# Around the expert loops of a two-block kernel: where the output store is awaited, where the gate is multiplied, and when the next weights are asked for

## The reference

```python
# each layer
x = x + gate_msa * attention(modulate(rms_norm(x)))
h = modulate(rms_norm(x))
g_idx = argmax(h @ w_group + b_group)                 # one group of 8 experts
top_v, top_i = top_k(e_logits[g_idx], 2)              # two experts inside it
weights = g_prob[g_idx] * softmax(top_v)              # w1, w2 per token
# expert_dispatch: assignments sorted by expert, padded to blocks
hid = silu(xb @ w_gate[e]) * (xb @ w_up[e])           # 1024 -> 512
ys  = hid @ w_down[e]                                 # 512 -> 1024
y[token] = w1 * ys[slot1] + w2 * ys[slot2]
x = x + gate_mlp * y
# after both layers
out = rms_norm(x) * final_norm_g
```

## Time and profile before

| | |
|---|---|
| median of 3 runs | 2659.88 us (2655.5 to 2660.84) |
| the profiled execution, its time | 2657.06 us |
| its span, first to last instruction | 2655.1 us |
| PE busy | 2244.2 us, 85% of the span |
| PEld busy | 996.6 us, 38% |
| DVE busy | 591.2 us, 22% |
| ACT busy | 563.8 us, 21% |
| POOL busy | 184.6 us, 7% |
| mean granted TensorE clock | 0.923 of full speed |
| HBM traffic | 235 GB/s over the span |

### The profile page before, as it was taken

One profiled execution on the slowest core, in us unless ns is written; L12 is line 12 of the kernel. 1 busy time (PEld: TensorE's weight loads), 2 busy tenths in 40 slices (PEclk: granted clock), 3 DMA queues, 4 the chain that ended last, 5 costly groups with the idle time before them and its releaser, 6 DMA issues. The chain is left out here.

```text
span 2655.1 us, 21739 instructions
## 1 busy us (share of the span) xinstructions
PE 2244.2 (85%) x8350; PEld 996.6 (38%) x8350; DVE 591.2 (22%) x1288; ACT 563.8 (21%) x932; POOL 184.6 (7%) x364
## 2 busy tenths in 40 slices
PE   8999999999999987848887787499799488878782
PEld 4454544444444444422222222244454222222220
DVE  2364421221020055310000000210562200100003
ACT  2223310010020043211111111200781111112111
POOL 3130020000000012010000000100120100000001
PEclk9999999999999998868889999799899588899996
DMA  7478649113222030159999999610003399999994
GB/s 246 166 264 302 225 162 390 47 63 106 84 80 90 0 127 16 64 217 429 428 428 429 427 429 422 223 63 0 32 17 134 142 427 429 428 428 428 429 429 165
DMA packets 133673, 624.84 MB, mean 235 GB/s; under 512 B 14212, under 2 KB 25868, under 8 KB 109036
## 3 DMA queue, kind: packets, MB, share of 16 engines
q1 hardware_dynamic: 114912, 557.11, 52.1%
q0 software_dynamic: 13488, 49.86, 5.0%
q10 hardware_dynamic: 5212, 17.05, 1.6%
HBM read 571.31 MB, written 52.67 MB: 235 GB/s over the span
## 5 line engine op out<-in xcount | busy, mean ns | idle before, releaser
L1754 PE MATMUL ps<-ring,arena 128*64 128x512 f32 x2048 | 516.0, 666 | 134.7 <-ACT arena L1782 115.4
L221 PE MATMUL ps<-hT,ring 128*128 128x512 f32 (+3 forms) x1328 | 560.3, 584 | 4.2 <-issue 4.2
L221 PEld LDWEIGHTS ps<-hT,ring 128*128 128x128 f32 (+1 forms) x1328 | 249.2, 190 | 313.6 <-issue 309.7
L1754 PEld LDWEIGHTS ps<-ring,arena 128*64 128x64 f32 x2048 | 160.7, 153 | 468.3 <-issue 387.8
L1769 PE MATMUL ps<-ring,arena 128*64 128x512 f32 x1024 | 238.4, 620 | 31.7 <-ACT arena L1789 31.7
L228 PE MATMUL ps<-ring,hT 128*128 128x512 f32 x576 | 254.0, 600 | 3.3 <-ACT hT L189 1.6
L228 PEld LDWEIGHTS ps<-ring,hT 128*128 128x128 f32 x576 | 109.9, 193 | 137.4 <-issue 134.7
L1812 DVE TENSOR_TENSOR arena<-ps,arena 128x512 f32<-128x512 f32 x32 | 22.1, 692 | 604.2 <-PE ps L1754 604.2
L1066 PE MATMUL ps<-ring,arena 128*128 128x512 f32 x336 | 144.8, 592 | 0.8 <-issue 0.8
L1769 PEld LDWEIGHTS ps<-ring,arena 128*64 128x64 f32 x1024 | 81.6, 142 | 166.4 <-issue 129.2
L155 ACT ACTIVATE arena<-x 128x1024 f32<-128x1024 f32 x32 | 33.8, 1056 | 313.4 <-DVE x L1126 132.4
(11 more groups left out here) (332 smaller groups left out, 2060.4 us busy)
## 6 DMA issues: line engine op xcount, KB each, us to landing
ring<-in_expert_w_gate SPq DMA_DIRECT2D x64, 2048.0 KB, 16.7
ring<-in_expert_w_down SPq DMA_DIRECT2D x64, 2048.0 KB, 19.7
ring<-in_expert_w_up SPq DMA_DIRECT2D x64, 2048.0 KB, 19.6
ring<-in_ada_w SPq DMA_DIRECT2D x24, 2048.0 KB, 12.1
arena<-token_slots SPq DMA_DIRECT2D x32, 512.0 KB, 22.8
output_slots<-arena ACTq DMA_DIRECT2D x32, 512.0 KB, 10.2
token_slots<-arena POOLq DMA_DIRECT2D x1, 12288.0 KB, 44.6
output_slots<-arena POOLq DMA_DIRECT2D x1, 12288.0 KB, 80.3
```

Source lines behind the costliest of these rows:

```text
L221: mm = pe.matmul(out, w[:, c, cols], x[:, c, :], start=(c == 0), stop=(c == chunks - 1))
L1754: mm = pe.matmul(k.ps[slots, 2 + kind, :], k.xT[:, c, slots], w[:, c, :], start=(c == 0), stop=(c == KD - 1))
```

## The change

- Store behind the barrier: the wait for the last store and `all_stored` move from the end of the loop's part to the start of the next (`all_stored_vector`); POOL waits for it ahead of the gathers. `y_stored` and DVE's register with the number of pairs now live across the parts.
- Gate row in the loop: DVE alone moves the down output, 1024 columns, and multiplies it with `k.gate_m`; ACT's copy and its semaphore go. DVE waits for `gate_ready` ahead of the loop, POOL no longer at its end.
- Fused combination: x = w1 * y1 + x, x = w2 * y2 + x, both on DVE; ACT's part goes. The combination of tile tt + 1 stands ahead of tile tt's norm, and ACT loads the table of the root at the start of the part.
- Wider ranks: the sums share a stationary operand over several tiles, with 32 to 128 columns each; the counts become a fifth column group of the same bank.
- The next weights: SP no longer asks for `stream2` in the first part. In the middle part it waits for all gathers, asks for pieces 0 to 7, and then for the router's weights.

```diff
 def router_tensor(pe, k, m):
     pe.wait_ge(m.chosen, 1)
-    for tt in range(TT):
-        for src in range(tt + 1):
-            lhs = k.before if src == tt else k.ones
-            pe.matmul(k.ps[:, 1, tt * E:(tt + 1) * E], lhs[:, :], k.sel[:, src, :], start=(src == 0), stop=(src == tt))
+    rank = k.ps[:, 1, 0:(TT + 1) * E].rearrange("p (t e) -> p t e", t=TT + 1)
+    pe.matmul(rank[:, 0, :], k.before[:, :], k.sel[:, 0, :], start=True, stop=True, skip_group_check=True)
     for src in range(TT):
-        mm = pe.matmul(k.ps[:, 2, 0:E], k.ones[:, :], k.sel[:, src, :], start=(src == 0), stop=(src == TT - 1))
+        mm = pe.matmul(rank[:, src + 1:TT + 1, :], k.ones[:, :], k.sel[:, src:src + 1, :].to_broadcast([P, TT - src, E]),
+                       start=(src == 0), stop=(src == TT - 1), skip_group_check=True)
+        if src == 0:
+            pe.matmul(rank[:, 1:TT, :], k.before[:, :], k.sel[:, 1:TT, :], start=False, stop=False, skip_group_check=True)
     mm.then_inc(m.ranked, 1)
...
 def moe_scalar(act, k, m):
...
-        act.wait_ge(m.downed, i + 2)
-        act.wait_ge(m.y_stored, i * 16 + 1)
-        act.copy(k.ys[:, 0:512], k.ps[:, 5, :]).then_inc(m.y_act, 1)
-        act.wait_ge(m.y_act, i + 2)
         act.wait_ge(m.y_dve, i + 2)
         act.dma_start(k.y_slots[bass.ds(i * P, P), :], k.ys[:, :]).then_inc(m.y_stored, 16)
...
-def moe_vector(dve, k, m):
-    n = pair_count(dve, k, m)
+def moe_vector(dve, k, m, a):
+    n = k.pairs[a.lends] = pair_count(dve, k, m)
+    dve.wait_ge(a.gate_ready, 2)
...
-        dve.tensor_copy(k.ys[:, 512:1024], k.ps[:, 6, :]).then_inc(m.y_dve, 1)
-    dve.wait_ge(m.y_stored, n * 16 + 1)
-    dve.memset(k.all_stored[:, :], 0.0)
+        dve.tensor_tensor(k.ys[:, :], k.ps[:, 5:7, :].rearrange("p b c -> p (b c)"), k.gate_m[:, :], ALU.mult).then_inc(m.y_dve, 1)
...
 def combine_gpsimd(pool, k, cb):
 
+    pool.wait_ge(cb.stored, 1)
...
-def combine_scalar(act, k, cb, tt):
-
-    act.wait_ge(cb.gathered[tt], 32)
-    y1 = k.yg[:, 2 * tt, :]
-    act.activation(y1, y1, ACT.Copy, scale=k.route("w1")[:, tt, :]).then_inc(cb.weighed, 1)
+def all_stored_vector(dve, k, cb):
+
+    dve.wait_ge(cb.y_stored, cb.pairs * 16 + 1)
+    dve.memset(k.all_stored[:, :], 0.0).then_inc(cb.stored, 1)
...
 def combine_vector(dve, k, cb, ch, tt):
 
     dve.wait_ge(cb.gathered[tt], 32)
-    y1, y2 = k.yg[:, 2 * tt, :], k.yg[:, 2 * tt + 1, :]
-    dve.wait_ge(cb.weighed, tt + 1)
-    ch.link(dve.scalar_tensor_tensor(out=y1, in0=y2, scalar=k.route("w2")[:, tt, :], in1=y1, op0=ALU.mult, op1=ALU.add))
-    ch.link(dve.tensor_tensor(y1, y1, k.gate_m[:, :], ALU.mult))
-    dve.tensor_tensor(k.x[:, tt, :], k.x[:, tt, :], y1, ALU.add).then_inc(cb.x_ready, 1)
+    x, y1, y2 = k.x[:, tt, :], k.yg[:, 2 * tt, :], k.yg[:, 2 * tt + 1, :]
+    ch.link(dve.scalar_tensor_tensor(out=x, in0=y1, scalar=k.route("w1")[:, tt, :], in1=x, op0=ALU.mult, op1=ALU.add))
+    dve.scalar_tensor_tensor(out=x, in0=y2, scalar=k.route("w2")[:, tt, :], in1=x, op0=ALU.mult, op1=ALU.add).then_inc(cb.x_ready, 1)
     dve.wait_ge(cb.x_ready, tt + 1)
...
     if l == 1:
...
-    pool.wait_ge(a.gate_ready, 2)
...
-            n_pairs, used = moe_sync(sp, k, m, a)
-            for n in range(RING):
-                if n % 2 == 0:
-                    sp.wait_ge(used[n // 2], n_pairs + 1)
-                k.stream2.load(sp, n)
+            moe_sync(sp, k, m, a)
...
 def middle_part(nc, k, w):
...
+            for tt in range(TT):
+                sp.wait_ge(cb.gathered[tt], 32)
+            for n in range(8):
+                a.stream.load(sp, n)
             router_loads(sp, k, w, m, 1)
-            for n in range(RING, 8):
-                a.stream.load(sp, n)
             moe_sync(sp, k, m, a)
...
         def _(act):
+            act.preload_act_table(ACT.Sqrt)
             for tt in range(TT):
-                combine_scalar(act, k, cb, tt)
                 squares_scalar(act, k, norm1, tt, x_ready)
...
             ch = Chain(dve, chain)
+            all_stored_vector(dve, k, cb)
+            combine_vector(dve, k, cb, ch, 0)
             for tt in range(TT):
-                combine_vector(dve, k, cb, ch, tt)
+                if tt + 1 < TT:
+                    combine_vector(dve, k, cb, ch, tt + 1)
                 scaled_vector(dve, k, norm1, tt)
                 turned_vector(dve, k, norm1, tt)
```

More of the change, by code:

```diff
@@ L1645, in router_vector @@
     dve.wait_ge(m.ranked, 1)
-    ch.link(dve.tensor_copy(f("count"), k.ps[:, 2, 0:E]))
+    ch.link(dve.tensor_copy(f("count"), k.ps[:, 1, TT * E:(TT + 1) * E]))
     ch.link(dve.tensor_tensor(f("cmp"), f("count").unsqueeze(2).to_broadcast([P, E, 8]),
@@ L1762, in moe_tensor @@
         pe.wait_ge(m.down_landed, i * 32 + 32)
-        pe.wait_ge(m.y_act, i + 1)
         pe.wait_ge(m.y_dve, i + 1)
@@ L1775, in moe_scalar @@
     n = pair_count(act, k, m)
-    act.sem_inc(m.y_act, 1)
     act.sem_inc(m.y_stored, 1)
@@ L2243, in layer_semaphores @@
      m.x_turned, m.xT_act, m.xT_dve, m.gate_landed, m.up_landed, m.down_landed, m.gated, m.upped, m.downed, m.hidden,
-     m.silu, m.h_turned, m.hT_out, m.y_act, m.y_dve, m.y_stored, m.slots_set) = semaphores(
+     m.silu, m.h_turned, m.hT_out, m.y_dve, m.slots_set) = semaphores(
         nc, f"moe{l}_", """router_landed logits diffs exps chosen ranked routed scattered x_landed x_turned xT_act
-        xT_dve gate_landed up_landed down_landed gated upped downed hidden silu h_turned hT_out y_act y_dve
-        y_stored slots_set""")
+        xT_dve gate_landed up_landed down_landed gated upped downed hidden silu h_turned hT_out y_dve
+        slots_set""")
+    m.y_stored = k.y_stored[l]
     m.w_gate, m.w_up, m.w_down = (w[n][l] for n in ("expert_w_gate", "expert_w_up", "expert_w_down"))
@@ L2253, in layer_semaphores, with combine_semaphores @@
     return a, m
-def combine_semaphores(nc, l):
+def combine_semaphores(nc, k, l):
     cb = Kit()
-    cb.weighed, cb.x_ready = semaphores(nc, f"combine{l}_", "weighed x_ready")
+    cb.y_stored, cb.pairs = k.y_stored[l], k.pairs[l]
+    cb.x_ready, cb.stored = semaphores(nc, f"combine{l}_", "x_ready stored")
     cb.gathered = [nc.alloc_semaphore(name=f"combine{l}_gathered{t}") for t in range(TT)]
@@ L2449, in _ @@
             router_vector(dve, k, m, ch)
-            moe_vector(dve, k, m)
+            moe_vector(dve, k, m, a)
 def middle_part(nc, k, w):
-    cb = combine_semaphores(nc, 0)
+    cb = combine_semaphores(nc, k, 0)
     chain, = semaphores(nc, "middle_", "dve_chain")
@@ L2508, in _ @@
             router_vector(dve, k, m, ch)
-            moe_vector(dve, k, m)
+            moe_vector(dve, k, m, a)
 def last_part(nc, k, w, out):
-    cb = combine_semaphores(nc, 1)
+    cb = combine_semaphores(nc, k, 1)
     chain, stored = semaphores(nc, "last_", "dve_chain stored")
@@ L2558, in two_block_kernel @@
         k.stream1, k.stream2 = (Stream(k, [ctx.enter_context(nc.semaphore(f"ring{i}_{n}")) for n in range(RING)]) for i in range(2))
+        k.y_stored, k.pairs = [ctx.enter_context(nc.semaphore(f"y_stored{l}")) for l in range(2)], [None, None]
         plan_first_block(k, w)
```

## The result

The changed kernel takes 2629.77 us, median of 4 runs (2625.41 to 2633.41), the kernel before 2658.1 beside it (2655.5 to 2660.84): ratio 0.9893, 95% interval 0.9873 to 0.9912. Faster by 1.1%, as forecast, and 0.8 us from the predicted 2629. In a later comparison it took 2629.82 against 2657.47. Its executions differ by some us: one took 2625.41 us at a mean granted clock of 0.930, three 2629.07 to 2633.41 us at 0.924. The profiled execution took 2629.07, its span is 2627.3 us.

What follows compares the result with a forecast made beforehand. It took DMA transfers to bound the two expert loops, after first turns at TensorE's pace, and waits their ends. Gains 6.8 + 9.1 + 13.4 = 29.3 us from 2657.06 gave 2627.8, moved halfway toward the median: 2629; range 2622 to 2641.

Steps and rivals of the forecast that it cites:

- Ranks: Rank matmuls before each expert loop: 16 fewer instructions at 0.214 us save 3.4 us per layer, 6.8 in all.
- My lower bound: Rank matmuls: if columns add to the weight load, 256 more cost 0.85 us, leaving 2.57 per layer, 5.1 in all.
- Gate in the loop: Expert loops: DVE's multiply makes the store 0.53 us later per turn; costed at nothing, hidden by 13.6 MB of transfers.
- TensorE's own pace goes from 30.73 to 31.26: Expert loops: TensorE's turn grows to 31.26 us, still under the mean of 31.36 that the transfers allow.
- The rival in which a longer gap costs more slow clock: Expert loops: the 0.53 us longer gap brings another 2.5 us clock loss, turns take 33.8, total 2696 us; chance 0.04.
- Store and barrier: End of first loop: the store's landing, not the barrier, decides; first gather at 1667.3 instead of 1676.32.
- Gathers, then weights: Middle part: weights asked for after all gathers; TensorE starts at 1689.4 instead of 1698.48, 9.1 us gained, bounds 3.8 to 10.5.
- +14.0: Middle part: all eight gathers landed 14.0 us after the first, from 8.78 us of issue and 5.2 until landing.
- the six loads did not land together: Middle-part rival: all six loads land together, 12.6 MB in 29.4 us, projection start 14.9 us later, 2653 us; chance 0.05.
- End of the kernel: Last part: earlier first gather and a chain set by DVE alone end at 2637.8 against 2651.21, 13.4 us gained.
- DVE without waits for ACT: Last part's chain: expected sign that DVE never waits for ACT, with a tile period of 4.4 us.
- Rule against the change: Middle part: the skill's rule, issue early and wait late, would with free gathers gain 14 us instead of 9; no term.

Runs made afterwards that it cites:

- the undone edit: The changed kernel with the 14 narrow rank matmuls of before: 2637.44 us against 2629.82 for the changed kernel beside it.
- the run with six early pieces: The changed kernel with six pieces of the next layer's weights asked for at the end of the first part again: 2637.72 us.
- the late request alone: The kernel before, with only the next weights asked for behind all gathers, router loads behind them: 2649.24 us, ratio 0.9965.

## Why the prediction was right

- **Ranks:** right to 0.1 us in each profile: 3.4 us per layer. The width adds nothing: 12 instructions of 32 to 128 columns in 2.8 us, 28 of 32 columns in 6.2, both at a granted clock of 0.50. My lower bound was mis-sized. An instruction of 512 columns takes 0.22 us at full clock (7.09 us for 32), so 256 more columns in each of two instructions cost 0.44 us at half clock, not 0.85: the bound is 6.0 us in all, not 5.1. By the rule of the Trainium skill (TensorE: Matmul & The Clock Gate, Back-to-back issue gap) the sum would then have been 0.9 us smaller (an estimate from this row), not 1.7; the 3.40 us per layer and the undone edit (7.6 us) do not show that either.
- **Gate in the loop:** the cost of nothing was right, the reason given for it only in part. The step "TensorE's own pace goes from 30.73 to 31.26" failed: the early turns stayed at 30.73 and settled there without transfers too. The clock took back 0.4 of 0.5 us. The transfers do cover later turns. With twice the multiply the cover is no longer whole: the 14 turns of the first loop take 2.8 us more. The rival in which a longer gap costs more slow clock did not come: the stretch of half clock was 6.8 us per turn before and after.
- **Store and barrier:** first gather 4.59 us behind the multiply, forecast 4.4. "SP's issues hold the barrier" is shown by the run with six early pieces, and the late request alone moves the gather by 7.1.
- **Gathers, then weights:** the mechanism right, the size off by 1.5 (7.6 gained at the first job instead of 9.1). The step "+14.0" measured 14.99 (1662.51 to 1677.50): the last gather was issued at +8.90 and landed 6.1 later, the upper end of my 4.3 to 6.3. The first piece took 8.4 instead of 8.1, so the six loads did not land together. The first two jobs lie 0.5 us further apart, for which I had no term. So 7.1 gained at the second job instead of 9.1.
- **End of the kernel:** 12.4 instead of 13.4. Tile 0 was there at +6.70, not +6.55, DVE waited 0.88 us for tile 1, which the sum had at once, and the period was 4.46 for 4.44. "DVE without waits for ACT" holds but for 0.28 us per tile, the root, which lies within the 0.6 of small steps.
- **Rule against the change:** the Trainium skill's advice to issue early (DMA: Bandwidth & Descriptors, Rules for kernel authors) is right here for the two pieces needed first and wrong for all six. I costed what obedience would give (14 us of gain instead of 9) and did not see that the idle DMA engines ahead of the store make most of it free: with two pieces early and the order of tiles the median is 10 us lower, and the profiles tie 7.8 of them to these two edits (projection at 27.97, then 20.2 us behind the multiply).
- **The number:** that it was only 0.8 us off is luck. The sum was 3.1 too large; 1.5 came from the start ahead of the router, which no term stood for, and I had added 1.2 for a median before of 2659.88, which in the comparison was 2658.1.

## What to carry to other kernels

A request for a later stage is not free just because its data are needed late: look whether its issue stands ahead of a barrier, and which transfer of the path shares the engines. Ask early for what fits the idle time of the engines and late for the rest. At a boundary, put the wait for a store behind the barrier, so that both run side by side, and order the tiles so that no engine of a chain waits for another.

## What the runs showed of the hardware

The granted clock of TensorE can hold a loop's pace. Four kernels of different work in a turn (copies or multiply, whole or half weights) settled at turns of 30.72 us, with 6.8 us of half clock in each; those with whole weights only in their early turns, before the transfers held them up. In the changed kernel the half clock begins at about 1250.3, in the 4.12 us in which TensorE idles ahead of its gate matmuls: a later start of the matmuls behind the gap meant fewer of them in the slow stretch. With 1.14 us more per turn (the second multiply) the turn varied between 31.0 and 32.6 us in a cycle of four, and its mean of 31.6 was 0.9 longer: the clock took back a quarter of a microsecond there, and no longer the whole. A delay of half a microsecond in such a loop can so cost nothing with no other cover in sight, and a gain of that size can bring nothing. What fixes the places of the slow stretches is not shown.
